# One core, two decoder blocks: the gated delta rule rewritten in 35 slots, and weights in halves with the high products first

## The chip, the cores and the metric

The kernel runs on one core of one Trainium2 chip. The metric is the device time of one execution in microseconds (us). The core's engines are TensorE (PE, with its weight loads as PEld), VectorE (DVE), ScalarE (ACT), GpSimd (POOL) and SyncE (SP), which issues the weight transfers.

## The reference

A sequence of 256 tokens of width 2048 goes through a hybrid layer (sparse attention beside a gated delta rule, then an MLP), and through a second block with a forgetting attention and a retention layer. Everything is float32. The change lies in the gated delta rule (GDN, 8 heads of 128, chunks of 64), and in how every large product takes its weights:

```python
def gated_delta_rule(q, k, v, g, beta):          # q, k, v: silu of a causal conv of width 4
    q = l2_normalize(q) * dk ** -0.5
    k = l2_normalize(k)
    ...
    g = jnp.cumsum(g, axis=-1)                   # in each chunk of 64
    kb = k * beta[..., None]; vb = v * beta[..., None]
    decay = where(tri, exp(g[:, None] - g[None, :]), 0)
    lower = where(strict, (kb @ k.T) * decay, 0)
    tinv = inverse(eye + lower)
    u = tinv @ vb
    w = tinv @ (kb * jnp.exp(g)[..., None])
    qk = (q @ k.T) * decay
    def step(state, inp):                        # over the 4 chunks
        v_new = un - wn @ state
        o = (qn * exp(gn)) @ state + qkn @ v_new
        state = state * exp(g_last) + (kn * exp(g_last - gn)).T @ v_new
```

The result is then normalized over its 128 columns, scaled by `norm_w`, and multiplied by `silu(z)`.

## The kernel before

**Large products.** All weights pass through one pipeline of *jobs*. A job is 256 tokens times a 2048 x 512 block of weights, and has 8 *granules* of 256 weight rows. A float32 product is made of three fp32r products: activations and weights are split into a high and a low part (`lt[0]`, `lt[1]`; `w_hi`, `w_lo`), and high x high, high x low and low x high are added up in PSUM (`acc`). For a granule, SP brings the rows into `raw` (four slots of 512 rows, 1 MB each, a slot for two granules), ACT writes `w_hi` (`split_hi`), DVE writes `w_lo = raw - w_hi` (`split_lo`), and PE issues 12 matmuls of 512 columns (`multiply`: 2 row blocks x 2 token tiles x 3 products). `w_hi` and `w_lo` hold four granules, so ACT may write granule r+4 once PE has done granule r. SP may refill a slot once DVE has taken both its granules (`lo_ready`).

**The mix.** Work of other kinds is cut by hand into generators (`mix`), one for each engine. PE takes one step of its generator ahead of each granule, ACT and DVE one ahead of each split of the granule four later. Such a place is called a *slot* here: in slot s PE does its mix step s and then granule s; ACT does step s and then `w_hi` of granule s+4; DVE does step s and then `w_lo` of granule s+4. Each engine goes through this in program order, so a PE step that needs the DVE step of the slot before waits, and the granule behind it waits too.

**GDN.** It is done for two groups of 4 heads (x 2 token tiles = 8 tiles of 128 x 128), beside jobs J_GDN+4 to J_GDN+7 (group 0) and J_MERGE to J_MERGE+3 (group 1), 32 slots each; the four jobs after these have no mix. Tiles are held in `arena` (SBUF) and come from PE through `mx`, four banks of PSUM. In a group PE turns the q, k, v projections into columns (L1490), DVE does the conv (L2021, ACT its first tap), ACT the silu, PE turns all back to rows (L1517), DVE normalizes q and k and scales them (up to L2059), PE turns q, k and the scaled q into columns again (L1532), makes the decay grid (L1539), k.k (L1545) and k.q (L1552). The triangular inverse takes 6 levels, in which both the inverse (`g_Y`) and its transpose (`g_X`) are updated: per level a product P = masked A x Y (L1563), then X x P (L1569) and P x X (L1572), with DVE updates between (L2096, L2098, L2101). The scan over 4 chunks follows (L1593, L1596, L1601, L1606; DVE L2112, L2117), in which PE waits for DVE inside a step, then the norm (L2131 to L2138, its root on POOL, L426), and the turn to columns for the next job (L337).

Of the kernel before, what the change touches and what calls it, by code (L numbers as in the profile page):

```python
# [20 lines left out]
ALU = mybir.AluOpType  # L21
# [112 lines left out]
def build(nc, x, rel_table, ln1_w, w_in, pe_k, pe_v, w1_k, w2_k, w1_v, w2_v, conv_w, a_log, dt_bias,  # L134
# [4 lines left out]
    with ctx:  # L139
# [66 lines left out]
        raw_loaded = [sem(f"raw_loaded{i}") for i in range(CPJ)]  # L206
# [23 lines left out]

        def load_job(sp, J, src, rows=512, chunks=CPJ):

            J = lin(J)
            for q in range(chunks):

                wait(sp, lo_ready, J * GPJ + 2 * q + 2 - GPJ)
                w = src(q)
                sp.dma_start(raw[:, q, :, :].rearrange("p a b -> p (a b)").rearrange(
                    "p (j n) -> p j n", j=rows // P), w.rearrange("(j p) n -> p j n", p=P)) \
                    .then_inc(raw_loaded[q], 16)  # L240
# [10 lines left out]
        def split_hi(act, J, r0, r1):  # L251

            J = lin(J)
            for r in range(r0, r1):
                slot, half = (r % GPJ) // 2, r % 2
                if half == 0:
                    wait(act, raw_loaded[slot], (J + (1 + r // GPJ)) * 16)

# [16 lines left out]
        def multiply(pe, J, lt, par, hook=None, mix=None, fresh=None):  # L275
# [6 lines left out]
            for r in range(GPJ):  # L282
# [3 lines left out]
                if fresh is not None:  # L286
                    wait(pe, lt_lo_ready, fresh + r + 1)
                wait(pe, lo_ready, J * GPJ + r + 1)
                for k in range(2):
                    kt = 2 * r + k  # L290
                    hi, lo = w_hi[:, r % 4, k, :], w_lo[:, r % 4, k, :]
                    for t in range(NT):
                        a_hi = lt[0][:, kt, t * P:(t + 1) * P]
                        a_lo = lt[1][:, kt, t * P:(t + 1) * P]
                        o = acc[par][t][:, :]
                        nc.tensor.matmul(o, a_hi, hi, start=(kt == 0), stop=False)  # L296
                        nc.tensor.matmul(o, a_hi, lo, start=False, stop=False)  # L297
                        last = nc.tensor.matmul(o, a_lo, hi, start=False, stop=(kt == KT - 1))  # L298
# [285 lines left out]
        g_z = at(3072, NT, NB)  # L584
        g_ct = at(4096, 12, 260)
        g_cv = at(7216, 12, S)
        g_rn = at(10288, NT, 12, HD)
        g_mask = at(13360, LEVELS + 3, P)
        M_STRICT, M_TRI, M_ONES = LEVELS, LEVELS + 1, LEVELS + 2
        g_sq = at(4096, NT, 8, HD)  # L590
        g_vb, g_kbeg, g_kdec = (at(i * 1024, NT, HG, HD) for i in range(3))
        g_qg = at(4096 + 2048, NT, HG, HD)
        g_qT, g_kT, g_qgT = (at(7216 + i * 1024, HG, S) for i in range(3))
        g_dec, g_qkT, g_A = (at(10288 + i * 1024, HG * NT, P) for i in range(3))
        g_X, g_Y, g_P1 = (at(4096 + i * 1024, HG * NT, P) for i in range(3))
# [94 lines left out]
        def _(sp):  # L690
# [63 lines left out]
        def _(pool):  # L754
# [50 lines left out]
            load(g_mask[:, :, :], c_masks[0:LEVELS + 3].rearrange("m p c -> p m c"), "mask_loaded")  # L805
            with fori(2) as g:
                root_pool(pool, sg("gss_ready"), Lin(1, [(2, g)]),
                          gss.rearrange("p a b -> p (a b)"), grs.rearrange("p a b -> p (a b)"), 16,
# [43 lines left out]
        def _(act):  # L852
# [147 lines left out]
            def gdn_mix(g):  # L1000
# [31 lines left out]
                for _ in range(3):  # L1032
                    yield
# [1539 lines left out]
```

## Time and profile before

| | us |
|---|---|
| median of 3 runs | 2958.01 (2956.99 to 2962.77) |
| the profiled execution's own time | 2958.05 |
| its span (first to last instruction) | 2956.4 |
| busy: PE, DVE, ACT | 2839.4, 1650.9, 1306.7 |
| mean granted TensorE clock | 0.983 of full speed |

The span is what the trace shows; 1.65 us lie around it. A busy PE is not a PE at its peak: matmuls overlap, so that their rate is read from the distance of two starts, not from a duration.

### The profile page before, as it was taken

Reading aid. Unit: us, or ns where it says so; the run is one execution under the profiler, and the core shown is the slowest. Engines: PE = TensorE matmul, PEld = TensorE weight load, DVE = VectorE, ACT = ScalarE, POOL = GpSimd, SP = SyncE. Lnnn points to the kernel's source line nnn. Section 1 sums busy time; section 2 is a strip of 40 time slices with the busy share of each in tenths; the row PEclk is TensorE's granted clock in tenths of the full one; section 3 lists DMA queues with packets and bytes.
Section 4 is the critical chain, followed back from the end, with each engine's and each line's share of the span. In section 5 each row is a group of like instructions: output and inputs, shape, how many; then the busy total and the mean of one; then the engine's idle time right before and its main releaser. Section 6 shows DMA issues by size and latency. Waiting matters only on the chain.

```text
span 2956.4 us, 34417 instructions
## 1 busy us (share of the span) xinstructions
PE 2839.4 (96%) x13554; PEld 2365.9 (80%) x13554; DVE 1650.9 (56%) x1884; ACT 1306.7 (44%) x1626; POOL 64.6 (2%) x65
## 2 busy tenths in 40 slices
PE   8999898899999999999999999999989999999997
PEld 7778786787878888888888888888878888888886
DVE  5555755645565555545555656556557555555556
ACT  5554534423434444434444454444444444344442
POOL 1000000000000000000000000000000000000000
PEclk9999999999999999999999999999989999999998
DMA  8754422314565655565565669679645555555563
GB/s 229 232 166 141 137 70 77 110 58 157 185 215 188 193 192 186 185 198 186 187 195 183 185 148 165 175 156 171 208 150 176 186 173 185 189 183 179 182 208 134
DMA packets 254025, 504.38 MB, mean 171 GB/s; under 512 B 8536, under 2 KB 17016, under 8 KB 252992
## 3 DMA queue, kind: packets, MB, share of 16 engines
q1 hardware_dynamic: 250512, 488.80, 54.2%
q0 software_dynamic: 3216, 13.59, 1.8%
q8 instruction: 101, 1.65, 0.2%
q14 instruction: 36, 0.29, 0.0%
q10 hardware_dynamic: 160, 0.04, 0.0%
HBM read 498.72 MB, written 3.67 MB: 170 GB/s over the span
## 4 chain that ended last, share of the span: by engine, by line
PE 75%; issue 20%; DMA 2%; DVE 1%; ACT 1%; POOL 1%; ACTq 0%; DVEq 0%; POOLq 0%
PE acc L296 22%; PE acc L298 22%; PE acc L297 22%; DMA bias_by_distance<-arena 1%; PE mx L337 1%; PE acc L1658 1%; PE acc L1656 1%; PE acc L1657 1%; DMA arena<-bias_by_distance 0%; POOL sm L426 0%; ACT w_hi L260 0%; ACT arena L500 0%; DVE w_lo L268 0%; DMA res<-in_x 0%; PE mx L1736 0%
## 5 line engine op out<-in xcount | busy, mean ns | idle before, releaser
L268 DVE TENSOR_TENSOR w_lo<-raw,w_hi 128x1024 fp32r<-128x1024 f32 x924 | 1133.1, 1227 | 1159.5 <-ACT w_hi L260 1146.0
L260 ACT ACTIVATE w_hi<-raw 128x1024 fp32r<-128x1024 f32 x924 | 979.2, 1060 | 1462.2 <-PE acc L298 1388.9
L296 PE MATMUL acc<-w_hi,lt_b_hi 128*128 128x512 f32 x1792 | 708.0, 395 | 2.9 <-DVE lt_b_lo L2360 2.5
L298 PE MATMUL acc<-w_hi,lt_b_lo 128*128 128x512 f32 x1792 | 698.9, 390 | 0.0
L297 PE MATMUL acc<-w_lo,lt_b_hi 128*128 128x512 f32 x1792 | 698.3, 390 | 0.0
L296 PE MATMUL acc<-w_hi,lt_a_hi 128*128 128x512 f32 x1696 | 674.9, 398 | 7.2 <-DVE w_lo L268 7.2
L298 PE MATMUL acc<-w_hi,lt_a_lo 128*128 128x512 f32 x1696 | 665.7, 393 | 0.0
L297 PE MATMUL acc<-w_lo,lt_a_hi 128*128 128x512 f32 x1696 | 665.4, 392 | 0.0
L296 PEld LDWEIGHTS acc<-w_hi,lt_b_hi 128*128 128x128 f32 x1792 | 337.1, 188 | 73.1 <-DVE lt_b_lo L2360 2.9
L298 PEld LDWEIGHTS acc<-w_hi,lt_b_lo 128*128 128x128 f32 x1792 | 336.9, 188 | 71.0
L297 PEld LDWEIGHTS acc<-w_lo,lt_b_hi 128*128 128x128 f32 x1792 | 337.3, 188 | 69.8 <-issue 1.9
L296 PEld LDWEIGHTS acc<-w_hi,lt_a_hi 128*128 128x128 f32 x1696 | 322.3, 190 | 73.5 <-issue 5.3
L298 PEld LDWEIGHTS acc<-w_hi,lt_a_lo 128*128 128x128 f32 x1696 | 321.6, 190 | 68.6
L297 PEld LDWEIGHTS acc<-w_lo,lt_a_hi 128*128 128x128 f32 x1696 | 322.4, 190 | 64.8
L353 DVE TENSOR_TENSOR lt_a_lo<-mx,lt_a_hi 128x512 fp32r<-128x512 f32 (+1 forms) x64 | 41.2, 685 | 34.6 <-ACT lt_a_hi L345 34.6
L426 POOL TENSOR_TENSOR sm<-sm 128x2 f32<-128x2 f32 (+2 forms) x17 | 22.3, 1313 | 1699.1 <-DVE sm L420 829.8
L345 ACT ACTIVATE lt_a_hi<-mx 128x512 fp32r<-128x512 f32 (+1 forms) x64 | 34.6, 593 | 52.8 <-PE mx L337 52.8
L1656 PE MATMUL acc<-w_hi,lt_b_hi 128*128 128x512 f32 x128 | 50.1, 391 | 0.0
L1658 PE MATMUL acc<-w_hi,lt_b_lo 128*128 128x512 f32 x128 | 49.8, 389 | 0.0
L1657 PE MATMUL acc<-w_lo,lt_b_hi 128*128 128x512 f32 x128 | 49.8, 389 | 0.0
L337 PE MATMUL mx<-ident,arena 128*128 128x128 f32 x280 | 38.1, 281 | 9.0 <-DVE arena L2138 9.0
L337 PEld LDWEIGHTS mx<-ident,arena 128*128 128x128 f32 x280 | 33.9, 145 | 14.2 <-DVE arena L2138 9.9
(355 smaller groups left out, 1726.4 us busy)
## 6 DMA issues: line engine op xcount, KB each, us to landing
raw<-in_ret_w_in SPq DMA_DIRECT2D x96, 1024.0 KB, 5.1
raw<-in_w_in SPq DMA_DIRECT2D x84, 1024.0 KB, 5.0
raw<-in_w_up SPq DMA_DIRECT2D x64, 1024.0 KB, 5.3
raw<-in_w_down SPq DMA_DIRECT2D x64, 1024.0 KB, 5.1
raw<-in_fox_w_in SPq DMA_DIRECT2D x64, 1024.0 KB, 7.7
raw<-in_ret_w_out SPq DMA_DIRECT2D x34, 1024.0 KB, 5.1
raw<-in_w_o SPq DMA_DIRECT2D x16, 1024.0 KB, 5.1
raw<-in_fox_w_out SPq DMA_DIRECT2D x16, 1024.0 KB, 5.1
```

Of the source, the lines that this page charges most:

```text
L260: nc.scalar.activation(w_hi[:, r % 4], raw[:, slot, 2 * half:2 * half + 2, :], ACT.Copy).then_inc(hi_ready, 1)
L268: nc.vector.tensor_tensor(w_lo[:, r % 4], raw[:, slot, 2 * half:2 * half + 2, :], w_hi[:, r % 4].bitcast(F32), ALU.subtract) \
L296: nc.tensor.matmul(o, a_hi, hi, start=(kt == 0), stop=False)
L297: nc.tensor.matmul(o, a_hi, lo, start=False, stop=False)
L298: last = nc.tensor.matmul(o, a_lo, hi, start=False, stop=(kt == KT - 1))
L337: last = nc.tensor.transpose(mx[:, b % 4, (2 * c + t) * P:(2 * c + t + 1) * P], src(2 * b + c, t), ident[:, :])
L345: nc.scalar.activation(dst(b)[0], mx[:, b % 4, :].rearrange("p (c s) -> p c s", s=S), ACT.Copy).then_inc(lt_hi_ready, 1)
L353: nc.vector.tensor_tensor(lo, mx[:, b % 4, :].rearrange("p (c s) -> p c s", s=S), hi.bitcast(F32), ALU.subtract).then_inc(lt_lo_ready, 1)
L426: nc.gpsimd.tensor_tensor(dst, base, mhalf[:, 0:w], ALU.pow).then_inc(done, 1)
L1656: MM(o, a_hi, w_hi[:, r % 4, k, :], start=(kt % 8 == 0), stop=False)
L1657: MM(o, a_hi, w_lo[:, r % 4, k, :], start=False, stop=False)
L1658: last = MM(o, a_lo, w_hi[:, r % 4, k, :], start=False, stop=(kt % 8 == 7))
```

## The change

1. *Weights in halves.* SP issues two transfers of 256 rows (512 KB) in place of one of 512 rows, each as soon as DVE has taken the granule that lay there; there are 8 semaphores in place of 4.
2. *High products first.* For a granule PE waits for `w_hi`, issues the 8 products with it, then waits for `w_lo` and issues the 4 products with it. The number of matmuls is the same.
3. *GDN.* q and k stay as columns after the silu; they aren't normalized themselves, but their norms are multiplied into rows of the results (`T_A`, `T_W`, `T_V`, `T_Q`), so the 24 turns of L1532 go. Only the inverse is updated by DVE; its transpose comes from a PE turn in each level. The first of 6 levels needs no product, only one turn of A. The first chunk of the scan, whose state is zero, has no product with the state.
4. *Slots.* A group takes 35 slots, and group 1 follows group 0 directly, through the jobs up to J_PAB. Products are put a slot or more ahead of the step that needs DVE's answer: a level takes two slots, a scan step two.

```diff
 def load_job(sp, J, src, rows=512, chunks=CPJ):
     for q in range(chunks):
-        wait(sp, lo_ready, J * GPJ + 2 * q + 2 - GPJ)
-        sp.dma_start(raw[:, q, :, :]..., w...).then_inc(raw_loaded[q], 16)
+        for half in range(2):
+            wait(sp, lo_ready, J * GPJ + 2 * q + half + 1 - GPJ)
+            sp.dma_start(raw[:, q, 2 * half:2 * half + 2, :]..., w[:, half * m:(half + 1) * m, :]) \
+                .then_inc(raw_loaded[2 * q + half], 16)
 def multiply(pe, J, lt, par, hook=None, mix=None, fresh=None):
+    wait(pe, hi_ready, J * GPJ + r + 1)
+    for k in range(2):
+        for t in range(NT):
+            for p in range(2):
+                nc.tensor.matmul(acc[par][t], lt[p][...], w_hi[:, r % 4, k, :], ...)
     wait(pe, lo_ready, J * GPJ + r + 1)
     for k in range(2):
         for t in range(NT):
-            nc.tensor.matmul(o, a_hi, hi, ...)
-            nc.tensor.matmul(o, a_hi, lo, ...)
-            last = nc.tensor.matmul(o, a_lo, hi, ...)
+            last = nc.tensor.matmul(acc[par][t], lt[0][...], w_lo[:, r % 4, k, :], ...)
     last.then_inc(granules_done, 1)
```

The generator of PE for a group, with every `yield` (the end of a slot's step):

```diff
+def gdn_mix(g):                       # PE; 8 tiles in each loop over h, t
+    columns(0); yield                                  # slot 0: turn k
+    columns(1); yield                                  # 1: turn q
+    columns(2); yield                                  # 2: turn v
+    (g == 0: sums of g) ; yield                        # 3
+    wait(gct_copied); MM(high, g of the tile, M_TRI); yield    # 4: decay grid
+    wait(gcum_ready, silu_done); natural(0); yield     # 5: turn k back
+    yield                                              # 6
+    wait(gb_taken); MM(high, k, k); yield              # 7
+    yield; yield; yield                                # 8, 9, 10
+    wait(a_ready); TR(high, g_A); natural(1); yield    # 11: waits for silu_done of q
+    wait(gsq_ready); MM(low, k, q); yield              # 12
+    for l in range(1, LEVELS):
+        wait(inv_y); MM(high, g_A, g_Y); TR(low, g_Y); yield       # 13, 15, ..., 21
+        wait(inv_p1, inv_x_copied); MM(high, g_X, g_P1)
+        if l == LEVELS - 1: natural(2)
+        yield                                                      # 14, 16, ..., 22
+    wait(inv_y); MM(high, g_kbeg, g_Y); yield          # 23
+    wait(vb_ready); MM(low, g_Y, g_vb); yield          # 24
+    for n in range(4):
+        if n: wait(s_ready, ...); MM(w, S); MM(q, S); yield        # 26, 28, 30
+        wait(v_ready, ...); (n < 3: MM(kdec, V)); (n % 2: MM(qkT, V)); yield   # 25, 27, 29, 31
+    yield; yield                                       # 32, 33
+    wait(go_ready); turn(pe, B_OB + 2 * g, ...); yield # 34
 for g in range(2):
-    mix = gdn_mix(g); four jobs; wait(pe, go_ready, g + 1); turn(pe, B_OB + 2 * g, ...)
+mix = gdn_groups()                    # gdn_mix(0), then gdn_mix(1)
+for J in range(J_GDN + 4, J_PAB):
+    multiply(pe, J, lt_a, J % 2, mix=mix)
```

And what DVE does in the slots that the prediction goes through (`tap(n, w)` is four instructions on 128 x 256, all `TT` here are 128 x 1024 but for those marked):

```diff
+    TT(D_, high_ps, cum); copy(egl) -> gb_taken; STT(D_) -> gdiff_ready; yield       # 5
+    sum_squares(0) -> gss_ready; TT(g_kdec); yield                                   # 6
+    tap(1, 2); wait(grs_ready); three small TT; yield                                # 7
+    TT(g_kbeg); wait(gdecay_ready); TT(g_A, g_E, T_A); yield                         # 8
+    wait(gram_ready); TT(g_A, high_ps, g_A) -> a_ready; tap(1, 3) -> conv_done; yield # 9
+    TT(g_qkT, g_E, mask); TT(z8, z8, gnorm); yield                                   # 10
+    wait(inv_p); TT(g_P1, high_ps, mask(0)) -> inv_p1; TT(g_Y) -> inv_y; yield       # 11
+    ...
+    wait(inv_p); TT(g_P1, high_ps, mask(l)) -> inv_p1; (l in 2, 3, 4: tap(2, l - 1)); yield
+    wait(inv_u); TT(g_Y, g_Y, high_ps) -> inv_y; yield
+    ...
+    add_inner(1); yield                                                              # 31
+    sum_out(1) (TT, reduce, 128x512); TT, TS small -> gss_ready; yield               # 32
+    wait(grs_ready); small TT; TT(g_o, T_O); TT(g_o, z8) -> go_ready; yield          # 33
+    turn_lo(dve, B_OB + 2 * g, ...); yield                                           # 34
```

**Order on PE, one inversion level of group 0.** A name like `acc<-w_hi,lt_a_hi` is what is written and read; `mx<-arena` is a product of the mix, `mx<-ident,arena` a turn. Before, a level and the start of the granule behind it:

```order
L1563 MATMUL mx<-arena 128x128 x8
L1569 MATMUL mx<-arena 128x128 x4
L1572 MATMUL mx<-arena 128x128 x4
L1569 MATMUL mx<-arena 128x128 x4
L1572 MATMUL mx<-arena 128x128 x4
L296 MATMUL acc<-w_hi,lt_a_hi 128x512
L297 MATMUL acc<-w_lo,lt_a_hi 128x512
L298 MATMUL acc<-w_hi,lt_a_lo 128x512
```

After, the same level with the two granules behind its two parts (L294 are the products with `w_hi`, L300 those with `w_lo`):

```order
L1607 MATMUL mx<-arena 128x128 x8
L1613 MATMUL mx<-ident,arena 128x128 x8
L294 MATMUL acc<-w_hi,lt_a_hi 128x512
L294 MATMUL acc<-w_hi,lt_a_lo 128x512
...
L300 MATMUL acc<-w_lo,lt_a_hi 128x512 x4
L1620 MATMUL mx<-arena 128x128 x8
L294 MATMUL acc<-w_hi,lt_a_hi 128x512
```

The level has 16 products and 8 turns in two slots where it had 24 products in one, and the four products with `w_lo` have moved behind the eight with `w_hi`.

**Order on DVE, from the k.k product to the first level, group 0.** L268 (now L269) is `w_lo` and ends a slot's step. Before:

```order
L2078 TENSOR_TENSOR arena<-arena 128x1024
L2079 TENSOR_TENSOR arena<-arena 128x1024
L268 TENSOR_TENSOR w_lo<-raw,w_hi 128x1024
L2083 SCALAR_TENSOR_TENSOR arena<-mx,tg,arena 128x128 x8
L2086 TENSOR_TENSOR arena<-mx,arena 128x1024
L2089 TENSOR_TENSOR arena<-arena 128x512 x2
L268 TENSOR_TENSOR w_lo<-raw,w_hi 128x1024
```

After (slots 8 to 11; L2081 is a conv tap):

```order
L2127 TENSOR_TENSOR arena<-mx,tg 128x1024
L2129 TENSOR_TENSOR arena<-arena,tg 128x1024
L269 TENSOR_TENSOR w_lo<-raw,w_hi 128x1024
L2132 TENSOR_TENSOR arena<-mx,arena 128x1024
L2081 SCALAR_TENSOR_TENSOR arena<-arena,cwg 128x256 x4
L269 TENSOR_TENSOR w_lo<-raw,w_hi 128x1024
L2135 TENSOR_TENSOR arena<-arena 128x1024
L2138 TENSOR_TENSOR arena<-arena,gnorm 128x1024
L269 TENSOR_TENSOR w_lo<-raw,w_hi 128x1024
L2141 TENSOR_TENSOR arena<-mx,arena 128x1024
L2143 TENSOR_TENSOR arena<-ident,arena 128x1024
L269 TENSOR_TENSOR w_lo<-raw,w_hi 128x1024
```

The masks and the k.q part have left the way to the first level, and the last conv tap of q now stands between them.

**Order on DVE, end of group 0** (the last chunk's output, the norm and the last product ahead of the turn). Before:

```order
L2123 TENSOR_TENSOR arena<-mx,arena 128x512
L268 TENSOR_TENSOR w_lo<-raw,w_hi 128x1024
L2130 TENSOR_TENSOR arena<-arena 128x1024
L2131 TENSOR_REDUCE sm<-arena 128x8
L2132 TENSOR_SCALAR sm<-sm 128x8
L268 TENSOR_TENSOR w_lo<-raw,w_hi 128x1024
L2135 TENSOR_TENSOR arena<-arena,sm 128x1024
L268 TENSOR_TENSOR w_lo<-raw,w_hi 128x1024
L2137 TENSOR_TENSOR arena<-arena,gnorm 128x1024
L2138 TENSOR_TENSOR arena<-arena 128x1024
```

After:

```order
L2179 TENSOR_TENSOR arena<-mx,arena 128x512
L269 TENSOR_TENSOR w_lo<-raw,w_hi 128x1024
L2171 TENSOR_TENSOR arena<-arena 128x512
L2172 TENSOR_REDUCE sm<-arena 128x4
L2204 TENSOR_TENSOR sm<-sm,tg 128x8
L2205 TENSOR_SCALAR sm<-sm 128x8
L269 TENSOR_TENSOR w_lo<-raw,w_hi 128x1024
L2208 TENSOR_TENSOR tg<-sm,tg 128x8
L2209 TENSOR_TENSOR arena<-arena,tg 128x1024
L2211 TENSOR_TENSOR arena<-arena 128x1024
L269 TENSOR_TENSOR w_lo<-raw,w_hi 128x1024
```

The sum over squares is made for half the rows at a time, and the step that scales by the norm and the one that multiplies by silu(z) are now in one slot.

## Rows read from the trace of the kernel before

**Rows 1.** The page: busy time by engine, and the chain that ended last by engine.

```profile
PE 2839.4 (96%) x13554; PEld 2365.9 (80%) x13554; DVE 1650.9 (56%) x1884; ACT 1306.7 (44%) x1626; POOL 64.6 (2%) x65
...
PE 75%; issue 20%; DMA 2%; DVE 1%; ACT 1%; POOL 1%; ACTq 0%; DVEq 0%; POOLq 0%
```

**Rows 2.** Groups of instructions, whole span: count | busy us, mean ns | idle before, releaser.

```profile
L268 DVE TENSOR_TENSOR w_lo<-raw,w_hi 128x1024 fp32r<-128x1024 f32 x924 | 1133.1, 1227 | 1159.5 <-ACT w_hi L260 1146.0 <-DMA res<-in_x 8.6
...
L296 PE MATMUL acc<-w_hi,lt_a_hi 128*128 128x512 f32 x1696 | 674.9, 398 | 7.2 <-DVE w_lo L268 7.2
```

**Rows 3.** Timeline, PE, undisturbed job: start us, length us, line.

```profile
1252.60 0.39 PE L296 MATMUL acc<-w_hi,lt_a_hi 128*128 128x512 f32 x1
1252.82 0.39 PE L297 MATMUL acc<-w_lo,lt_a_hi 128*128 128x512 f32 x1
1253.05 0.39 PE L298 MATMUL acc<-w_hi,lt_a_lo 128*128 128x512 f32 x1
1253.28 0.39 PE L296 MATMUL acc<-w_hi,lt_a_hi 128*128 128x512 f32 x1
```

**Rows 4.** Timeline, PE: first instruction of the stage, first after it.

```profile
302.65 0.33 PE L1490 MATMUL mx<-ident,res 128*128 128x128 f32 x1
...
775.50 0.39 PE L1656 MATMUL acc<-w_hi,lt_b_hi 128*128 128x512 f32 x1
```

**Rows 5.** Groups on PE, 302.6 to 775.7.

```profile
L1563 PE MATMUL mx<-arena 128*128 128x128 f32 x192 | 26.7, 298 | 8.5 <-DVE arena L2089 8.5
...
L1601 PE MATMUL mx<-arena 64*128 64x128 f32 x64 | 9.2, 285 | 8.9 <-DVE arena L2112 8.9
...
L1532 PE MATMUL mx<-ident,arena 128*128 128x128 f32 x48 | 8.6, 348 | 14.0 <-DVE arena L2059 14.0
...
L337 PE MATMUL mx<-ident,arena 128*128 128x128 f32 x16 | 3.9, 428 | 9.0 <-DVE arena L2138 9.0
```

**Rows 6.** Timeline, PE, eight products of 128 columns and the next eight.

```profile
399.15 1.06 PE L1569 MATMUL mx<-arena 128*128 128x128 f32 x8
400.04 1.06 PE L1572 MATMUL mx<-arena 128*128 128x128 f32 x8
```

**Rows 7.** Stretches: us, busy time by engine (instructions), PEclk, DMA share, GB/s.

```profile
302.60:775.70 473.10, 417.81 (x2281) 358.32 (x2282) 268.56 (x389) 190.18 (x245) 12.83 (x5) 0.95 0.33 107
...
881.60:885.00 3.40, 3.40 (x10) 2.63 (x9) 3.11 (x4) 0.34 (x1) 0.00 (x0) 0.50 0.68 216
```

**Rows 8.** Groups on DVE and ACT, 302.6 to 775.7.

```profile
L2021 DVE SCALAR_TENSOR_TENSOR arena<-arena,cwg 128x256 f32<-128x256 f32 x72 | 30.1, 480 | 0.2
...
L2131 DVE TENSOR_REDUCE sm<-arena 128x8 f32<-128x1024 f32 x2 | 2.4, 1222 | 0.1
...
L2132 DVE TENSOR_SCALAR sm<-sm 128x8 f32<-128x8 f32 x2 | 0.3, 173 | 0.1
...
L1016 ACT ACTIVATE arena<-arena 128x1024 f32<-128x1024 f32 x6 | 6.3, 1058 | 3.0 <-DVE arena L2021 2.9
```

**Rows 9.** The page: the group of roots on POOL.

```profile
L426 POOL TENSOR_TENSOR sm<-sm 128x2 f32<-128x2 f32 (+2 forms) x17 | 22.3, 1313 | 1699.1 <-DVE sm L420 829.8
```

**Rows 10.** Timeline, PE: three granules that began late.

```profile
12.93 0.47 PE L296 MATMUL acc<-w_hi,lt_a_hi 128*128 128x512 f32 x1 [1.17 <-DVE w_lo L268]
...
81.02 0.50 PE L296 MATMUL acc<-w_hi,lt_a_hi 128*128 128x512 f32 x1 [3.02 <-DVE w_lo L268]
...
880.25 0.47 PE L296 MATMUL acc<-w_hi,lt_a_hi 128*128 128x512 f32 x1 [3.05 <-DVE w_lo L268]
```

**Rows 11.** DMA issues: KB each, median us from issue to landing.

```profile
raw<-in_ret_w_in SPq DMA_DIRECT2D x96, 1024.0 KB, 5.1
...
raw<-in_fox_w_in SPq DMA_DIRECT2D x64, 1024.0 KB, 7.7
...
out_x<-res SPq DMA_DIRECT2D x4, 512.0 KB, 2.8
...
arena<-c_rope POOLq DMA_DIRECT2D x1, 256.0 KB, 3.3
```

More of the change, by code:

```diff
@@ L290, in multiply @@
                     kt = 2 * r + k
-                    hi, lo = w_hi[:, r % 4, k, :], w_lo[:, r % 4, k, :]
                     for t in range(NT):
[L293 to L298, printed above, removed]
+                        last = nc.tensor.matmul(acc[par][t][:, :], lt[0][:, kt, t * P:(t + 1) * P],
+                                                w_lo[:, r % 4, k, :], start=False, stop=(kt == KT - 1))
                 last.then_inc(granules_done, 1)
@@ L1032, in gdn_mix @@
[L1032 to L1042 removed]
+                hs = g * HG
@@ L1083, in _ @@
+            assert next(mix, "over") == "over"
             for n in range(4):
@@ new lines, in gdn_mix @@
+                for h in range(HG):
+                    for t in range(NT):
+                        last = MM(tile(2, h, t), tok[:, G_G, t, hs + h:hs + h + 1].to_broadcast([P, P]),
+                                  g_mask[:, M_TRI, :], start=True, stop=True)
+                last.then_inc(sg("gram_ready"), 1)
+                yield
+                pe.wait_ge(sg("gcum_ready"), 1)
+                pe.wait_ge(sg("gct_copied"), 6 * g + 4)
+                natural(0)
+                yield
+                yield
@@ new lines, in gdn_mix @@
+                pe.wait_ge(sg("gb_taken"), g + 1)
+                for h in range(HG):
+                    for t in range(NT):
+                        k = g_k[:, h, t * P:(t + 1) * P]
+                        last = MM(tile(2, h, t), k, k, start=True, stop=True)
+                last.then_inc(sg("gram_ready"), 1)
+                yield
+                yield
+                yield
+                yield
+                pe.wait_ge(sg("a_ready"), g + 1)
+                for h in range(HG):
+                    for t in range(NT):
+                        last = TR(tile(2, h, t), g_A[:, h, t, :], ident[:, :])
@@ L2145, in _ @@
             assert next(mix, "over") == "over"
-            for g in range(2):
-                mix = gdn_mix(g)
-                for kind in range(4):
-                    splits((J_GDN + 4 if g == 0 else J_MERGE) + kind, mix)
-                assert next(mix, "over") == "over"
-                turn_lo(dve, B_OB + 2 * g, part(lt_b, NH + g * HG), 2)
-            with fori(2) as i:
-                for c in range(2):
-                    splits(Lin(J_MERGE + 4 + c, [(2, i)]))
+            mix = gdn_groups()
+            for J in range(J_GDN + 4, J_PAB):
+                splits(J, mix)
+            assert next(mix, "over") == "over"
             dve.wait_ge(acc_taken[0], (J_PAB + 1) // 2)
```

683 lines of the change are left out of this document (357 added, 326 removed).

## The prediction

> **What bounds the kernel now.** I read the page's busy times first, then the chain, the groups of instructions, and last single stretches of the timeline. PE is busy for 96% of the span and makes 75% of the chain; DVE has 56% and ACT 44% [rows 1]. DVE sits idle ahead of `w_lo` until ACT has written `w_hi` (1146 us in all), and PE waits for `w_lo` only 7.2 us in its dearest group [rows 2]. So PE sets the time, and two things can change it: what PE is given to do, and the places where it waits.
>
> The rate of its work is the distance of two starts, not the 398 ns of one matmul [rows 2]. In an undisturbed job the starts are 0.23, 0.22, 0.23 and 0.23 us apart [rows 3]: from 1252.60 to 1253.28 three matmuls take 0.68, 0.227 each, so a granule of 12 takes 2.72 us. The 128-column instructions of the mix are 0.89 us apart for eight [rows 6], 0.111 each. In the trace a product of the mix appears as two such instructions, a turn as one (192 instructions of L1563 for 2 groups x 6 levels x 8 products; 48 of L1532 for 2 x 24 turns) [rows 5].
>
> The GDN stage lasts from 302.65, the first turn, to 775.50, where J_PAB begins [rows 4]: 472.9 us for 12 jobs. It holds 2281 PE instructions, one of them J_PAB's [rows 7]. 96 granules x 12 are 1152, which leaves 1128 of the mix. 96 x 2.72 = 261.1 us and 1128 x 0.111 = 125.2. PE is idle for 473.1 - 417.8 = 55.3 us [rows 7], nearly all until DVE has answered: 14.0 ahead of the second turn of q and k, 9.0 ahead of the turn to the next job, 8.9 inside the scan, 8.5 ahead of the first level [rows 5]. What is left, 472.9 - 261.1 - 125.2 - 55.3 = 31.3, is time at half clock and small losses at each change between granule and mix. The granted clock over the stage is 0.95 [rows 7], where 1.00 is 2.4 GHz and 0.50 is 1.2. 5% of 473 us is 24 us of full clock missing, some of it while PE idled. I put 24 on the clock and 7 on the changes, of which there are some 42 slots with a mix: 0.17 us a slot.
>
> **What the change does to the stage.** *PE's instructions.* By the new generator a group has: turns of columns 24, turns back 24, turn of A 8, turns of Y 5 x 8 = 40, last turn 8, together 104; products: grid, k.k and k.q 24, levels 5 x 16 = 80, w and u 16, scan 3 x 8 + 3 x 4 + 2 x 4 = 44, together 164, at two instructions each 328. That is 432 a group, 864 for two, and 8 for the sums: 872, where there were 1128. 872 x 0.111 = 96.8 us, 28.4 less. The granules stay 261.1.
>
> *Waits.* I follow the slots. Let T(s) be when PE begins slot s. Granule s-1 has just ended, ACT needs 1.06 us for a `w_hi` and DVE 1.22 for a `w_lo` [rows 2, 8], and with the 0.16 that the last matmul's end lies behind its distance, DVE begins its step s at T(s) + 2.44 if it isn't late. A 128 x 1024 instruction of DVE takes 1.22, a tap 30.1 / 72 x 4 = 1.67, a small one 0.17 [rows 8].
> - Levels. In a slot with X x P, PE's product ends at T + 1.8, DVE's update runs from T + 2.44 to 3.66, and PE needs it at T + 1.8 + 2.72 = 4.52: 0.86 to spare. In the other slot P is ready at 3.66 and needed at 1.8 + 0.9 + 2.72 = 5.4; with a tap behind it DVE ends at 5.3 and its `w_lo` at 6.6, still ahead of its next start at 5.4 + 2.44. No wait. So the scan: `s_ready` at T + 3.1 at slot 25 against 3.6, later slots with more.
> - Slot 11. DVE has 2.6, 2.6, 2.2, 2.4 and 2.9 us in slots 5 to 9 and four `w_lo` between, 17.6 in all, so the last tap of q ends at T(5) + 2.4 + 17.6 = 20.0, and ACT's silu at 21.1. PE has 0.9 + 1.8 of mix and six granules up to T(11), 19.0, and the turn of A, 19.9. It waits 1.2 us; I take 1.5 a group, 3 us.
> - Slot 34. DVE begins the last sum of squares at T(32) + 2.4 and needs 0.7 + 0.7 + 0.3; the root on POOL takes 1.3 [rows 9], which is T(32) + 5.4 or T(33) + 2.7; then 0.2 + 1.2 + 1.2 gives T(33) + 5.3, where PE is there at 2.72. It waits 2.6, with the semaphores on the way 3, for two groups 6 us. Before it waited 4.5 a group at this place (L337).
>
> Together 9 us of the 55. The former waits of L1532, L1563 and L1601 go: the first has no successor, the second is moved to slot 11, the third has its answer a slot away.
>
> *Clock and changes.* A wait of 3.05 us at 880.25 was followed by 3.4 us at 0.50 [rows 7, 10], a loss of 1.7. I expect it after both waits of slot 34 and once more: 5 us. 58 slots with a mix x 0.17 = 10.
>
> The stage then takes 261.1 + 96.8 + 9 + 5 + 10 = 382 us, 91 less.
>
> **High products first.** Where `w_lo` is in time the order costs nothing by the rows: a matmul follows at 0.227 whether the stationary operand is the same (L296 to L297), new (L297 to L298), or new together with the PSUM bank (L298 to L296) [rows 3]; the new order holds these steps and no others but the new bank with a w_lo operand. That could cost from nothing to something I can't bound, and I take nothing. Where `w_lo` is late, PE can have up to 8 x 0.227 = 1.8 us of work first. It is late three times: 1.17 us at 12.93, 3.02 at 81.02, 3.05 at 880.25 [rows 10]. The first goes (-1.2); at 81.02 `w_hi` was late too, PE begins when it is there, one `w_lo` (1.2) sooner; at 880.25 DVE had been held up long before, so 1.8 go. With some clock behind it, 5 us.
>
> **Weights in halves.** Over 900 transfers of 512 KB take the place of half as many of 1 MB. SP's issue isn't waited for. A granule's refill now begins up to a granule (2.7 us) sooner, and it is needed seven granules after it began to be free, 19 us; a full megabyte lands in 5.1 us, at worst kind 7.7 [rows 11]. Hidden work; 0 to 2 us of gain at 81.02, where weights were late. The cost of a half transfer lies between 2.8 us (512 KB out of `res`, same queue) and, by the step from 256 KB in 3.3 to 1 MB in 5.1, some 3.9 [rows 11]. That is more than the 2.72 of a granule, so it is hidden only as long as transfers overlap. They do: in the forgetting attention each takes 7.7 us, is issued for every 5.44 us of PE work, and all of PE's 7.2 us of waits for `w_lo` lie elsewhere [rows 2, 10].
>
> The Trainium skill, "DMA: Bandwidth & Descriptors", sections on the anatomy of one DMA and on bandwidth, speaks against this edit: it advises transfers of at least 1 MiB and gives about 2.0 us plus bytes at 436 GB/s for one (fitted on the path that GpSimd issues). By that a half costs 3.2 us (my estimate from the page), and if nothing overlapped, 0.48 us would be missing at each of 924 granules, 444 us in all. The rows for 7.7 us say that it overlaps, and no run so far shows halves.
>
> **Sum.** 2958 (the profiled execution's 2958.05, and the median 2958.01 is the same) - 91 - 5 = **2862 us**.
>
> **The rivals.**
> - *Forecast*, 2862, own range 2852 to 2874: chance 0.60.
> - *The slots are too tight.* The 0.86 to spare in a level is less than one DVE instruction, and DVE passes through `w_lo` in every slot. If the ten hand-overs of Y and ten others (slots 5, 23 to 31) wait 1.1 us each, as L1601 did (8.9 / 8), 22 us come back, and half clock behind them, 10 more: 2894. For it speaks that DVE falls behind in slots 5 to 9; against it that nothing queues up in the levels. 0.17.
> - *Better*: no half clock behind the waits of slot 34 (-5), the late weights at 81.02 gone (-2), slot 11 in time (-3): 2852. For it: a wait of 3 us need not be followed by half clock every time, and 256 rows land sooner than 512. 0.17.
> - *Slower: the transfers stop overlapping.* The place is every granule; the price is 924 x (time of a half - 2.72). It overtakes the 96 us of gain when a half costs over 2.82 us of the queue's time. At 2.8 it would be 2862 + 74 = 2936, at 3.9 the kernel takes 3950. Against it the overlap shown above. 0.04, of which 0.03 slower than before. By the page's 3.2 it would be 2862 + 444 = 3306.
> - *The change does not do what it says*: the order of products alone costs 9 ns a matmul in the steps not seen before (11,088 x 8.7 ns = 96 us), so nothing is won. 0.02, shared between no change and slower.
>
> A measurement of this kernel tells about 0.2% (6 us) from no change. Faster 0.95, within 0.2% 0.01, slower 0.04. The range reaches from the better case to near the tight one, with the 4 us of my rounding in the clock below it: 2848 to 2892.
>
> **What would show it.** In the profile after: a stage of 382 us, with 872 PE instructions of the mix; in the chain of waits, PE idle of about 3 us once a group ahead of the last turn and 1 to 2 ahead of the turn of q (slot 11), and none over 0.5 in the levels and the scan; starts still 0.227 apart in a job without a mix; PE's waits for `w_lo` gone at 12.93 and cut to about 1.2 near 880; weights landing in less than 5 us. The prediction is wrong if PE idles in the levels, if clean jobs take more than 21.8 us, or if `w_hi` waits for weights.

## The result, and the profile after

The changed kernel takes **2862.27 us** (median of 4 runs, 2859.95 to 2867.5), the kernel before 2957.51 on the same chip. The ratio is 0.9681, with a 95% interval of 0.9669 to 0.9693: 3.2% faster. The forecast was 2862 with a range of 2848 to 2892. The profiled execution took 2864.14 us, with a span of 2862.3 where it was 2956.4.

The page of the changed kernel: busy time by engine, and the chain that ended last.

```profile
PE 2792.8 (98%) x13298; PEld 2324.6 (81%) x13298; DVE 1611.4 (56%) x1785; ACT 1298.4 (45%) x1609; POOL 66.4 (2%) x67
...
PE 94%; DVE 2%; ACT 2%; issue 1%; DMA 1%; POOL 0%; ACTq 0%; DVEq 0%; POOLq 0%
```

PE has 13298 instructions where [rows 1] have 13554: 256 fewer, the count that the prediction made from the generator. It is 98% busy, and the chain is PE's for 94% (75% before). Its busy time fell by 46.6 us only, half of the 94.1 us by which the span fell; the other half was idle time.

Where the GDN stage begins and ends (timeline, PE, changed kernel; start us, length us, line):

```profile
300.04 1.09 PE L1535 MATMUL mx<-ident,res 128*128 128x128 f32 x8
...
680.85 0.39 PE L1712 MATMUL acc<-w_hi,lt_b_hi 128*128 128x512 f32 x1
```

The stage takes 380.8 us. By [rows 4] it took 472.9. So 92.1 of the span's 94.1 us come from here, 2.6 from the work ahead of it (it begins at 300.04, before at 302.65), and the work behind it is 0.6 us longer. The stage's busy times and counts (table by stretches, changed kernel; us, busy (instructions) of PE, PEld, DVE, ACT, POOL, granted clock, DMA share, GB/s):

```profile
300.00:681.00 381.00, 369.67 (x2025) 315.93 (x2026) 229.44 (x290) 181.04 (x227) 14.69 (x7) 0.99 0.46 134
```

2025 instructions, less 1152 of the granules and the one of J_PAB, are 872 of the mix, where there were 1128 [rows 7]. PE's idle time is 11.3 us (55.3 before), the clock 0.99 (0.95 before). PE's waits say what the 11.3 are. Some lines of the list over the whole kernel (engine, line, whom it waits for: us in all, times, longest; changed kernel):

```profile
...
PE mx L340 <- DVE arena L2211: 8.3, 2, 4.2
...
PE mx L1544 <- ACT arena L1030: 2.9, 2, 1.6
...
PE acc L294 <- issue: 2.5, 1, 2.5
...
PE acc L300 <- DVE w_lo L269: 0.9, 1, 0.9
```

L340 is the last turn of a group (slot 34), L1544 the turn that waits for q's silu (slot 11): two each, and these 11.2 us are all that the list has inside the stage: no line of the levels or of the scan stands in it. The 14.0, 8.9 and 8.5 us of [rows 5] have no successor in the list; the last turn, which had 9.0 there, has 8.3. `w_lo` is waited for once, 0.9 us (at 784), where [rows 10] have 1.17, 3.02 and 3.05. The other two lines lie behind the stage. In the wait "issue" PE waited for nothing that the profile shows; it is 2.5 us where the kernel before has 0.4.

### The profile page after: what moved, and what is told of

Read it like the earlier page. It is cut to its first block, busy times and chain, and to the rows that moved or that the text cites. A ratio compares the mean times of both kernels' runs of the same rounds, so it can differ in the third digit from the quotient of the medians.

```text
span 2862.3 us, 35850 instructions
## 1 busy us (share of the span) xinstructions
PE 2792.8 (98%) x13298; PEld 2324.6 (81%) x13298; DVE 1611.4 (56%) x1785; ACT 1298.4 (45%) x1609; POOL 66.4 (2%) x67
## 4 chain that ended last, share of the span: by engine, by line
PE 94%; DVE 2%; ACT 2%; issue 1%; DMA 1%; POOL 0%; ACTq 0%; DVEq 0%; POOLq 0%
PE acc L294 54%; PE acc L300 27%; PE mx L340 1%; PE acc L1714 1%; PE acc L1713 1%; PE acc L1712 1%; ACT w_hi L261 1%; ACT arena L503 1%; DVE w_lo L269 1%; PE mx L1620 1%; PE mx L1607 1%; PE mx L476 0%; PE mx L484 0%; PE mx L1613 0%; DMA res<-in_x 0%
## 5 line engine op out<-in xcount | busy, mean ns | idle before, releaser
L269 DVE TENSOR_TENSOR w_lo<-raw,w_hi 128x1024 fp32r<-128x1024 f32 x924 | 1133.6, 1228 | 1152.4 <-ACT w_hi L261 1138.6
L294 PE MATMUL acc<-w_hi,lt_b_hi 128*128 128x512 f32 x1792 | 708.6, 395 | 5.6 <-DVE lt_b_lo L2430 3.0
L294 PE MATMUL acc<-w_hi,lt_b_lo 128*128 128x512 f32 x1792 | 699.2, 390 | 0.0
L294 PE MATMUL acc<-w_hi,lt_a_hi 128*128 128x512 f32 x1696 | 673.8, 397 | 0.0
L294 PE MATMUL acc<-w_hi,lt_a_lo 128*128 128x512 f32 x1696 | 664.6, 392 | 0.0
L300 PE MATMUL acc<-w_lo,lt_b_hi 128*128 128x512 f32 x1792 | 480.7, 390 | 0.0
L300 PE MATMUL acc<-w_lo,lt_a_hi 128*128 128x512 f32 x1696 | 454.5, 390 | 0.9 <-DVE w_lo L269 0.9
L294 PEld LDWEIGHTS acc<-w_hi,lt_b_hi 128*128 128x128 f32 x1792 | 337.5, 188 | 76.8 <-issue 5.4
L300 PEld LDWEIGHTS acc<-w_lo,lt_b_hi 128*128 128x128 f32 x1792 | 337.4, 188 | 70.7
L294 PEld LDWEIGHTS acc<-w_hi,lt_b_lo 128*128 128x128 f32 x1792 | 337.5, 188 | 70.0 <-issue 1.9
L300 PEld LDWEIGHTS acc<-w_lo,lt_a_hi 128*128 128x128 f32 x1696 | 319.3, 188 | 68.4 <-DVE w_lo L269 1.3
L294 PEld LDWEIGHTS acc<-w_hi,lt_a_hi 128*128 128x128 f32 x1696 | 320.8, 189 | 66.2 <-issue 1.3
L294 PEld LDWEIGHTS acc<-w_hi,lt_a_lo 128*128 128x128 f32 x1696 | 320.9, 189 | 64.3
L429 POOL TENSOR_TENSOR sm<-sm 128x2 f32<-128x2 f32 (+1 forms) x19 | 24.3, 1279 | 1621.6 <-DVE sm L423 829.4
L1713 PE MATMUL acc<-w_lo,lt_b_hi 128*128 128x512 f32 x128 | 49.8, 389 | 0.0
L340 PE MATMUL mx<-ident,arena 128*128 128x128 f32 x280 | 37.2, 277 | 8.3 <-DVE arena L2211 8.3
L340 PEld LDWEIGHTS mx<-ident,arena 128*128 128x128 f32 x280 | 33.2, 142 | 13.5 <-DVE arena L2211 9.2
```

The source lines that it names most:

```text
L269: nc.vector.tensor_tensor(w_lo[:, r % 4], raw[:, slot, 2 * half:2 * half + 2, :], w_hi[:, r % 4].bitcast(F32), ALU.subtract) \
L294: nc.tensor.matmul(acc[par][t][:, :], lt[p][:, kt, t * P:(t + 1) * P], w_hi[:, r % 4, k, :], start=(kt == 0 and p == 0), stop=False)
L300: last = nc.tensor.matmul(acc[par][t][:, :], lt[0][:, kt, t * P:(t + 1) * P], w_lo[:, r % 4, k, :], start=False, stop=(kt == KT - 1))
L340: last = nc.tensor.transpose(mx[:, b % 4, (2 * c + t) * P:(2 * c + t + 1) * P], src(2 * b + c, t), ident[:, :])
L1713: MM(o, a_hi, w_lo[:, r % 4, k, :], start=False, stop=False)
```

## The experiments

All ratios are against the kernel before on the same chip. "The changed kernel" has 2862.27 beside 2957.51 for the kernel before; the chips of the experiments gave 2957.3 to 2958.6 for the kernel before, so a difference of medians between experiments is known to some 1.5 us at best. A trace shows one execution, and single traces differ by a few us in how long PE ran at half clock: between 20 and 300 us 10.2 us in the kernel before, 13.7 in the changed kernel, 17.1 in experiment 10.

**1. High products first alone.** The kernel before with one edit:

```diff
+    wait(pe, hi_ready, J * GPJ + r + 1); 8 matmuls with w_hi
     wait(pe, lo_ready, J * GPJ + r + 1)
-    12 matmuls (hi x hi, hi x lo, lo x hi by turns)
+    4 matmuls with w_lo
```

> The kernel before with one edit: the eight products with w_hi ahead of the four with w_lo. Theory (it only fills waits for w_lo): starts stay 0.227 us apart, the waits at 12.93 and 81.02 shrink by 1.2 us each, the one at 880 from 3.05 to about 1.2, the GDN stage stays at 472.9; 2953, 4 to 6 us less than before. Rival (the order makes matmuls dearer): each ns a matmul shows as 11 us more. Rival (it also shortens the stage, since PE may begin before w_lo): more than 10 us less.

Measured: 2954.07 us (before 2957.29), ratio 0.9986 (0.9977 to 0.9995). Near 81 us PE waits 1.7 for `w_hi` where it waited 3.02 for `w_lo`, and at 878 1.0 where it waited 3.05. The wait of 1.17 at 12.93 is gone. The 3.2 us by the medians are less than the 4 to 6 that were expected, but they go the expected way, and the steps between matmuls that no row had shown cost nothing that shows (9 ns each would have been 96 us).

**2. Halves alone.** The kernel before with transfers of 256 rows and 8 semaphores:

```diff
-        wait(sp, lo_ready, J * GPJ + 2 * q + 2 - GPJ); sp.dma_start(512 rows).then_inc(raw_loaded[q], 16)
+        for half in range(2):
+            wait(sp, lo_ready, J * GPJ + 2 * q + half + 1 - GPJ)
+            sp.dma_start(256 rows).then_inc(raw_loaded[2 * q + half], 16)
```

> The kernel before with one edit: transfers of 256 rows in place of 512. Theory (hidden by overlap): same within 0.1%, at most 2 us less where weights were late near 81; a half lands in under 5 us. Rival (a half costs 2.8 us or more of the queue's time): 70 us more or worse.

Measured: 2952.93 us (before 2957.29), ratio 0.9985 (0.9976 to 0.9994), 4.4 us by the medians. No fixed cost shows. By the medians the gain is larger than the 0 to 2 expected, though the interval reaches from 1.8 to 7.1. The wait of 3.02 us near 81 is gone altogether, because the weights were what was late there, while a wait of 5.4 us for `w_lo` stands at 873 in this trace. That is 2.4 more than before at that place, with DVE's order unchanged. The trace doesn't say where the 4.4 us come from: it is of the slowest of the eleven executions (2956.57), its span is 1.5 us shorter than before, the stage 3.1 us shorter (44 us at half clock in it in place of 51), the work ahead of it only 0.6, and the work behind it 2.2 longer.

**3. The changed kernel with whole transfers.** The reverse of experiment 2's edit, in the changed kernel.

> The changed kernel with 512-row transfers as before. Theory: 2862 to 2865, the wait for weights near 81 comes back in part. Rival (halves carry part of the gain): 2870 or more.

Measured: 2864.31 us, ratio 0.9679 (0.9666 to 0.9693). Halves give 2.0 us by the medians in the changed kernel, less than the intervals can tell from nothing; the stage takes 379.5 us, because one stretch at half clock at the last turn of group 0 is 3.4 us long in place of 6.8. Near 78 us PE waits 1.3 for `w_hi` again.

**4. The changed kernel with the old order of products.** The reverse of experiment 1's edit.

> The changed kernel with the three products of a tile side by side as before. Theory: the new slots need no early start, the stage stays at 381, the waits for w_lo at 12.9 and near 880 come back: 2867. Rival (the slots of GDN live on the early start): the stage grows by 5 us or more and the time passes 2872.

Measured: 2866.13 us, ratio 0.9693 (0.968 to 0.9706). The wait for `w_lo` near 782 is 2.9 in place of 0.9, with 3.4 us at half clock behind it, and 1.1 are back at 12.9. The stage is 380.8 us, as in the changed kernel.

**5. Both pipeline edits, GDN as before.** Experiments 1 and 2 in one kernel.

> The kernel before with both pipeline edits (halves, high products first) and the old GDN. Theory (the two add up: 3.9 and 4.2 us alone, with the late weights near 81 gained once only): 2949 to 2952, the GDN stage 470 to 473. Rival (the new GDN isn't what shortens the stage): below 2930.

Measured: 2949.58 us (before 2958.58), ratio 0.9970 (0.996 to 0.9979). Together 9.0 us, about the sum of 3.2 and 4.4. The stage takes 473.8 us (301.03 to 774.81), where it took 472.9: the two edits do nothing for it. The rest of the 95 us is the GDN's.

**6. Three slots more in each group.** The changed kernel with an empty step of each engine ahead of slot 11 and two ahead of slot 34, 38 slots:

```diff
 # PE                                     # ACT: one ahead of squares(1), two ahead of turn_hi
+    yield                                # DVE: one behind the product with z8, two ahead of turn_lo
     wait(a_ready); TR(high, g_A); natural(1); yield
 ...
+    yield; yield
     wait(go_ready); turn(pe, B_OB + 2 * g, ...); yield
```

> The changed kernel with three more empty slots in each group: one ahead of the turn of A, two ahead of the last turn (38 slots, 76 of 96 in use). The work is the same. Theory (PE waits only where an answer is a slot too far): the waits of 1.5 and 4.2 us, in all 11.5, go, with half clock behind them 3 to 5 more: 2846 to 2850. Rival (what is waited for there is bound by DVE's own work and only moves on): the waits come back in the slots behind and the time stays within 3 us of 2862.

Measured: **2848.34 us** (2958.58 before), ratio 0.9628 (0.9615 to 0.9642). The same table by stretches, of this kernel, over its whole stage:

```profile
300.90:665.80 364.90, 364.50 (x2025) 312.71 (x2026) 228.84 (x290) 184.44 (x230) 13.46 (x7) 1.00 0.47 140
```

The instructions are the same 2025; the idle time is 0.4 us and the clock 1.00, with no stretch at half clock. The stage is 16.0 us shorter for it: 10.9 of waits, and 5.1 for the 10.2 us at half clock that are gone with them. This is the fastest of all kernels here: 14 us under the changed one.

**7. The scan with one slot a step.** The changed kernel, in which the hand-overs of the scan lose their spare slot (32 slots in a group):

```diff
     wait(v_ready, ...); MM(kdec, V); ...
-    last.then_inc(scan_ready); yield          # PE; ACT and DVE lose the same yields
+    last.then_inc(scan_ready)
```

> The changed kernel with each of the three later scan steps in one slot instead of two (32 slots a group, the same instructions). Theory: PE waits 1.2 to 1.3 us for v_new in each of 6 steps as it did before, 7.5 us, half clock behind some of them 2 to 5, less 1 for six slots fewer with a change: 2869 to 2874. Rival (the early place buys nothing): within 2 us of 2862.

Measured: 2873.31 us, ratio 0.9717 (0.9703 to 0.973). PE's waits in this kernel's stage:

```profile
PE mx L340 <- DVE arena L2208: 8.4, 2, 4.2
PE mx L1657 <- DVE arena L2186: 5.0, 4, 1.3
PE mx L1543 <- ACT arena L1030: 3.2, 2, 1.6
PE mx L1662 <- DVE arena L2186: 2.6, 2, 1.3
PE mx L1590 <- DVE arena L2130: 1.4, 1, 1.4
```

Six waits of 1.2 to 1.3 us are back, as L1601 had them [rows 5], 7.6 us in all, and one of 1.4 at the turn of A. The stage is 12.0 us longer (392.8), with four stretches at half clock in it, 17.0 us in all, of which one (same table, this kernel):

```profile
416.80:420.20 3.40, 3.40 (x14) 2.98 (x13) 1.81 (x5) 0.00 (x0) 0.00 (x0) 0.50 0.37 138
```

PE works through the whole stretch, at 0.50, the lower of its two levels (1.2 GHz). The stretch begins 1 us after the end of one wait of 1.28 us (at 415.82), the first since 340.5. The next wait of the scan is followed by such a stretch too (1.22 us, then 427.1), and the four after it are not (1.28 at 434.4, 569.8 and 585.2, 1.21 at 577.9): the length of a short wait doesn't tell whether the clock falls.

**8. 256 more instructions on PE.** The changed kernel issues the grid, k.k, k.q, w and, in four levels, X x P twice over (with the same result each time), which makes 1128 instructions of the mix, as before:

```diff
-    for h in range(HG):
+    for h in 2 * list(range(HG)):
         for t in range(NT):
             last = MM(tile(2, h, t), ...)
```

> The changed kernel with 8 sets of 8 products of each group done twice in a row into the same place (grid, k.k, k.q, four of X x P, w): 256 more PE instructions of 128 columns, so that the stage has the 1128 of before in the new slots; the second time adds nothing to the result. Theory (instructions cost their distance, 0.111): 28 us more, 2890. Rival (they fill time in which PE idled): less than 20 us more.

Measured: 2890.16 us, ratio 0.977 (0.9756 to 0.9783). The stage by stretches, this kernel:

```profile
299.40:707.80 408.40, 397.60 (x2281) 344.38 (x2282) 230.42 (x290) 181.16 (x227) 12.56 (x7) 0.99 0.43 125
```

It takes 408.3 us, 27.5 more: 0.107 us an instruction, where the prediction used 0.111. Waits stay nearly as they are (8.4 at L340, 2.4 at L1544, which was 2.9), and so do the 10.2 us at half clock; with the 0.5 us less of waits an instruction is 0.109. The 2281 instructions are as many as in the kernel before [rows 7], which took 472.9: the other 64.6 us of the stage's gain are waits and half clock, and don't come from the number of PE's instructions. They come from the order together with DVE's smaller share in it (290 instructions and 229.4 us busy in the stage, 389 and 268.6 before); no run separates these two but for the scan (experiment 7).

**9. Transfers of a quarter.** The changed kernel with every transfer cut once more, to 256 KB; a semaphore is raised by both parts, and ACT waits for 32 in place of 16 a granule:

```diff
-            sp.dma_start(256 rows).then_inc(raw_loaded[2 * q + half], 16)
+            for i in range(2):
+                sp.dma_start(128 of them).then_inc(raw_loaded[2 * q + half], 16)
```

> The changed kernel with each transfer of 256 rows cut once more, into two of 128 rows (256 KB each, or halves of the columns where a granule is one row block), which raise the same semaphore. Theory (transfers overlap, so their size matters only for when a granule's weights are complete): no change within 0.2% of the changed kernel's 2862, so 2856 to 2868, PE's starts still 0.227 apart in a clean job, and PE waits for w_lo at no new place. Rival (each transfer has a fixed cost that doesn't overlap on the queue, or SP's issue becomes the bound): doubling the count at a fixed part of even 1 us beyond what is hidden gives hundreds of us more; w_hi then waits for weights in clean jobs. Between them: landing time is 3.6 to 4.7 us for 512 KB and 5.1 to 7.7 for 1 MB, so I expect 2.8 to 3.5 us for 256 KB, but the queue holds four transfers at a time in place of two or three.

Measured: 2861.91 us, ratio 0.9674 (0.9661 to 0.9687): the same as with halves, with over 1800 transfers. PE waits for `w_lo` once, 1.9 us, at the place where it waited 0.9, with 3.4 us at half clock behind it. What the queue shows, first with whole transfers (experiment 3; share of the 16 DMA engines' time, then what is loaded, count, size, us to landing):

```profile
q1 hardware_dynamic: 250512, 488.80, 55.7%
...
raw<-in_ret_w_in SPq DMA_DIRECT2D x96, 1024.0 KB, 5.0
```

with halves (changed kernel):

```profile
q1 hardware_dynamic: 257904, 488.83, 59.9%
...
raw<-in_ret_w_in SPq DMA_DIRECT2D x192, 512.0 KB, 3.7
...
raw<-in_fox_w_in SPq DMA_DIRECT2D x128, 512.0 KB, 4.7
```

with quarters (this experiment):

```profile
q1 hardware_dynamic: 272688, 488.89, 56.6%
...
raw<-in_ret_w_in SPq DMA_DIRECT2D x384, 256.0 KB, 2.8
```

From 5.0 over 3.7 to 2.8 us: a transfer of a quarter of the size lands in more than half of the time, so each has a part that doesn't shrink, some 2 us by a line through the three (an estimate). PE doesn't pay it: with four times as many transfers its time is the same, since others are under way meanwhile.

**10. Two slots more, ahead of the last turn alone.** The part of experiment 6 that aims at slot 34:

```diff
+    yield; yield                              # PE, ACT and DVE
     wait(go_ready); turn(pe, B_OB + 2 * g, ...); yield
```

> The changed kernel with two empty slots more, both ahead of the last turn of a group (slot 34 becomes 36), and slot 11 as it is. Theory: the waits of 4.18 and 4.17 us go, and with them 3.4 us at half clock behind one of them (1.7 lost); slot 11's waits of 1.58 and 1.37 stay, and the half clock at 448.9 in group 0, if it hangs on the last turn, goes as well. The stage takes 380.8 - 8.35 - 2 to 5 = 368 to 371 us, the kernel 2850 to 2853. Rival (the 16 us that three more slots gave come mostly from the room at slot 11, or from another spread of the mix over jobs): the stage stays above 375. This tells which of the added slots is worth it.

Measured: 2850.34 us, ratio 0.9636 (0.9623 to 0.9649); the stage takes 369.8 us (301.38 to 671.2). PE's waits, 250 to 800 us, of this kernel:

```profile
PE mx L1546 <- ACT arena L1030: 4.0, 3, 1.6
PE mx L484 <- ACT arena L503: 1.4, 2, 0.7
PE acc L300 <- DVE w_lo L269: 1.1, 1, 1.1
PE mx L1601 <- ACT arena L1035: 0.6, 1, 0.6
```

Both waits of L340 are gone, and no stretch of the stage is at half clock any more: 11.0 us for 8.35 of waits. (L484 lies ahead of the stage, and its 1.4 us are in the changed kernel too.) 12 of the 14 us of experiment 6 are these two slots. It isn't free elsewhere: group 1 now stands two granules later against the jobs, and waits of 0.8 and 0.6 us are new in it (at 497 and 501).

## Why the prediction was right, point by point

*What bounds it.* PE sets the time. Experiment 8 puts back what PE was relieved of and nothing else, and the stage gets 27.5 us of the prediction's 28.4 back. The 92.1 us of the stage are, by size: 44.0 of waits (55.3 to 11.3), 27.5 of instructions, and some 20 of half clock, if PE loses half of such a stretch (51 us in ten stretches of 3.4 or 6.8 between 349.1 and 690.4 before, 10.2 after). The prediction had 46, 28 and 19, less 3 for more changes. It named only 40.4 of the 55.3 us as its four waits for DVE and called that nearly all; the others were 6.2 ahead of the scan's first product (L1593), 3.0 ahead of turns that waited for ACT (L1517), 3.0 ahead of k.q (L1552) and 2.7 of small ones. They went as well, which the prediction's walk through the slots contained but didn't argue one by one.

*The stage's sum.* Each term against what the changed kernel's trace has:

| term, us | predicted | measured |
|---|---|---|
| granules | 261.1 | 261.1 (pitch as before) |
| 872 instructions of the mix, and changes between mix and granules | 96.8 + 10 = 106.8 | 103.4 (what is left over) |
| waits | 9 | 11.3 |
| half clock | 5 | 5 (half of 10.2) |
| stage | 382 | 380.8 |

The granules' pitch is read from a job without a mix: four starts from 1251.74 to 1252.42 lie 0.22 to 0.23 us apart. The half clock is read from the first two of these stretches (table by stretches for PE alone, changed kernel), 10.2 us; the third lies behind the stage:

```profile
448.90:455.70 6.80, 5.66 (x18) 0.50 0.28 82
605.90:609.30 3.40, 3.40 (x10) 0.50 0.55 154
1223.70:1227.10 3.40, 3.40 (x10) 0.50 0.24 90
```

Both in the stage lie at the last turn of a group, as the prediction placed them, but it had counted three of 3.4 us: the "once more" didn't come, and the first was twice as long, so that the 5 is right partly by luck. The stretch at 1223.70 is not in the prediction's sum. Instructions and changes can't be told apart in one trace: experiment 6, nearly free of waits, leaves 364.8 - 261.1 - 0.4 = 103.3 us for both as well. With experiment 8's 0.107 for an instruction it would be 93.3 and 10, so that the 3.4 us too much lie in the price of an instruction; with 0.109 it would be 95.0 and 8.3, and the price would be half of it. In the total these 3.4 us too much more than hide the 2.3 us by which the waits were put too low: the stage's total came out closer than its terms.

*Levels and scan.* "No wait" held for all of them. The margin of 0.86 us in a level was enough in each of the ten hand-overs of Y, and so was the room in the other places that the tight rival named. For the scan experiment 7 shows that the spare slot is what makes it so: without it the scan's waits come back at 1.2 to 1.3 us each.

*Slot 11.* Predicted 1.5 us a group, measured 1.58 and 1.37.

*Slot 34: the right place, the term mis-sized.* "It waits 2.6, with the semaphores on the way 3": it is 4.18 and 4.17. The timeline shows the step that is off (POOL, changed kernel; start, length, idle before):

```profile
444.73 2.54 POOL L429 TENSOR_TENSOR sm<-sm 128x8 f32<-128x8 f32 x1 [91.29 <-DVE sm L2205]
```

and DVE in the same kernel and place:

```profile
444.48 0.17 DVE L2205 TENSOR_SCALAR sm<-sm 128x8 f32<-128x8 f32 x1
444.56 1.22 DVE L269 TENSOR_TENSOR w_lo<-raw,w_hi 128x1024 fp32r<-128x1024 f32 x1
447.30 0.17 DVE L2208 TENSOR_TENSOR tg<-sm,tg 128x8 f32<-128x8 f32 x1 [1.53 <-POOL sm L429]
447.50 1.23 DVE L2209 TENSOR_TENSOR arena<-arena,tg 128x1024 f32<-128x1024 f32 x1
448.76 1.23 DVE L2211 TENSOR_TENSOR arena<-arena 128x1024 f32<-128x1024 f32 x1
```

and PE:

```profile
444.80 1.07 PE L300 MATMUL acc<-w_lo,lt_a_hi 128*128 128x512 f32 x4
450.05 1.97 PE L340 MATMUL mx<-ident,arena 128*128 128x128 f32 x8 [4.18 <-DVE arena L2211]
```

The root for 8 columns takes 2.54 us. I had taken 1.3 from [rows 9], whose line has a "128x2" in it and a mean over several shapes; the difference of 1.24 is the 1.2 that the wait came out longer. The trace of the kernel before had the right number, at the same step of group 0 (timeline, POOL):

```profile
485.17 2.54 POOL L426 TENSOR_TENSOR sm<-sm 128x8 f32<-128x8 f32 x1 [142.39 <-DVE sm L2132]
```

and for 128x2 it has 0.81 us in the mean (groups of the same kernel, different shapes kept apart; count | busy us, mean ns | idle before, releasers):

```profile
L426 POOL TENSOR_TENSOR sm<-sm 128x2 f32<-128x2 f32 x13 | 10.5, 809 | 1334.9 <-DVE sm L420 829.8 <-DVE sm L2450 338.4 <-DVE sm L2337 166.7
```

In the changed kernel PE had ended its granule at 445.87, DVE wrote the last product till 449.99, and the turn began at 450.05.

*High products first and halves.* -5 predicted for both, all of it outside the stage; the changed kernel's trace is 2.0 us shorter there (2.6 ahead of the stage, less 0.6 behind it), so this term was 3 us too large. Alone on the old GDN they gave 9.0 (experiment 5); on the new one, taken out one at a time, 3.9 and 2.0 (experiments 4 and 3), by medians whose intervals overlap with the changed kernel's; of the 3.9 the trace shows 2.0 as the longer wait near 782, 1.1 at 12.9, and 3.4 us at half clock (1.7 lost), though that one execution (2863.90) is no longer than the changed kernel's profiled one. In the trace the three waits for `w_lo` went as predicted or further: the one at 12.93 is gone, so is the one near 81, of which 1.8 was to stay, and near 784 0.9 us is left where 1.2 was expected. But ahead of the stage 4.2 us of waits went and only 2.6 arrive, since this trace has 3.4 us more at half clock there (1.7 lost). Behind the stage about 4 us were saved that don't show in the sum, because a wait of 2.51 us "issue" and 3.4 us at half clock came in later (timeline, PE, changed kernel):

```profile
1222.30 0.50 PE L294 MATMUL acc<-w_hi,lt_b_hi 128*128 128x512 f32 x1 [2.51 <-issue]
```

It stands two matmuls into the second pass of the program loop over the MLP's jobs, just behind the jump back to the loop's start. Such a wait of 2.0 to 3.6 us is in every kernel with the new GDN (in experiment 6 there are two, 0.95 and 3.2), and in the four kernels with the old one it is 0.3 to 0.5 us at this place (0.44 at 1317.80 before). In four of the eight with the new one 3.4 us at half clock follow (changed kernel, experiments 3, 6 and 8), in the others none. The profile shows no semaphore that was waited for, which speaks for a lack of instructions rather than of data; but that is only argued. Why only with the new code wasn't tested, and stays open.

*The total.* The profiled execution took 2864.14 us, 2.1 more than the 2862 predicted: the stage gave 1.1 more, the rest 3.0 less, and 0.2 more lie around the span. That the median of the four executions, 2862.27, comes within 0.3 is luck, as they lie between 2859.95 and 2867.5.

*Overlap of transfers.* The rival that they stop overlapping needed a half to cost more than 2.82 us of the queue. Halves take 3.6 to 4.7 us to land, more than that and more than the 2.72 of a granule, and the time didn't rise; so a landing time is no cost of the queue. The Trainium skill, "DMA: Bandwidth & Descriptors", sections on the anatomy of one DMA and on bandwidth, advises 1 MiB or more for each transfer, with 2.0 us of fixed cost. The fixed part agrees with the landing times (2 us by the line through three sizes), but its advice doesn't bind here: 1 MB, 512 KB and 256 KB gave 2864.3, 2862.3 and 2861.9 us, the same within their intervals.

## What to carry to other kernels

Where one engine sets the time and works through a written order of slots, count two things for each hand-over: what the other engines do between request and answer, and how much of the bounding engine's own work stands between. An empty slot cost nothing that shows as long as the stage had slots to spare (experiment 6 leaves the same 103.3 us for instructions and changes), and two of them in each group ahead of the slowest answer were worth 12 us, more than either pipeline edit. Look up the duration of a small operation in the shape that it will have: a group's mean over shapes mis-sized the wait at slot 34, where the trace of the kernel before had the right number. Transfers smaller than 1 MB cost nothing here, where several were under way; what they gave is an earlier start for what waits for the first part.

## What the hardware showed that I had not expected

- A root on POOL took 0.81 us in the mean for 128x2 and 3.36 for 128x16 (kernel before), and for 128x8 2.54 ahead of the last turn. The same shape took from 1.63 to 2.71 us at other places of the changed kernel's stage, so the shape alone doesn't give the duration.
- PE stood still for 2 to 3.6 us with no semaphore to wait for that the profile shows, just behind the first jump back of a program loop far from the edited GDN, in every kernel with the new GDN, and for 0.3 to 0.5 us there in those with the old. The cause is open.
- Waits can cost more than their length, through the clock: in experiment 7, 7.6 us of waits in the scan and 1.4 at the turn of A made the stage 12.0 us longer, with 17.0 us at a granted clock of 0.50 (at 416.8, 427.1 and 447.5 for 3.4 us, at 597.7 for 6.8) where the changed kernel has 10.2; in experiment 6 10.9 us of waits less gave 16.0 us.
